# Picking the rows of the ten small expert blocks on the chip instead of loading them

## What is computed

```python
def moe(h, w_router, b_router, w_gate, w_up, w_down):
    t = h.reshape(b * l, d)                       # 384 x 1024
    scores = jax.nn.sigmoid(t @ w_router)         # 16 experts
    ...                                           # best of 4 groups, top 2 in it -> gates
    hidden = jax.nn.silu(einsum('nd,edf->nef', t, w_gate)) * einsum('nd,edf->nef', t, w_up)
    out = jnp.einsum('nef,efd->nd', hidden * gates[..., None], w_down)
```

## Time and profile before

| | |
|---|---|
| runs of the kernel before | 1582.39, 1579.22, 1567.40 us, median 1579.22 us |
| span of the profiled execution | 1581.7 us |
| its own time | not given apart; the run nearest above the span is 1582.39 us, 0.7 us more |
| busy PE / DVE / ACT / POOL | 86% / 33% / 21% / 10% of the span |
| mean granted TensorE clock | 0.919 of full speed |
| DMA moved | 354.67 MB, mean 224 GB/s |

### The profile page before, as it was taken

How to read it: one execution, slowest core, us unless ns; L and a number is a source line. 1 busy time by engine, 2 the same in 40 slices (tenths; PEclk the granted TensorE clock), 3 DMA queues, 4 the chain that set the end, 5 groups by cost and what they waited for, 6 DMA issues and landing times.

```text
span 1581.7 us, 38798 instructions
## 1 busy us (share of the span) xinstructions
PE 1352.5 (86%) x16856; PEld 916.1 (58%) x16856; DVE 524.0 (33%) x1147; ACT 334.9 (21%) x665; POOL 164.3 (10%) x237
## 2 busy tenths in 40 slices
PE   4978899989889898899788759988899889987872
PEld 1446764458677755899444424445565579954441
DVE  1232453134344673311001024447455441110113
ACT  2222121032222313100000023423443210000001
POOL 2012220012231300100000012010000010000001
PEclk9997899999788998999989978998879899999996
DMA  9856426321110116589999985115313458999994
GB/s 396 317 175 203 145 84 248 129 107 56 55 56 4 56 54 276 206 326 391 385 396 401 417 318 221 54 69 213 139 75 160 170 185 309 401 385 399 403 416 169
DMA packets 42072, 354.67 MB, mean 224 GB/s; under 512 B 5675, under 2 KB 10619, under 8 KB 23632
## 3 DMA queue, kind: packets, MB, share of 16 engines
q1 hardware_dynamic: 21456, 302.11, 48.5%
q0 software_dynamic: 8672, 28.53, 5.3%
q10 hardware_dynamic: 11808, 22.03, 4.3%
HBM read 321.63 MB, written 31.01 MB: 223 GB/s over the span
## 4 chain that ended last, share of the span: by engine, by line
PE 66%; DMA 15%; DVE 8%; issue 7%; ACT 3%; SPq 1%; POOLq 0%; another core or an unknown queue 0%; DVEq 0%; ACTq 0%; POOL 0%
PE PB L647 60%; DMA arena<-in_w_moe 7%; DMA ring<-in_w_moe 6%; PE PB L650 5%; DVE arena L1948 4%; DMA ring<-in_w_mod 2%; ACT arena L1486 1%; DVE small L1961 1%; DVE x L1948 1%; DVE arena L1955 0%; SPq L413 0%; DMA arena<-expert_out,rows_i 0%; DVE arena L1958 0%; ACT L1486 0%; DVE hT L1951 0%
## 5 line engine op out<-in xcount | busy, mean ns | idle before, releaser
L647 PE MATMUL PB<-arena 64*64 64x64 f32 (+6 forms) x9564 | 506.8, 301 | 77.9 <-DMA arena<-in_w_moe 35.0
L647 PEld LDWEIGHTS PB<-arena 64*64 64x64 f32 (+3 forms) x9564 | 399.3, 135 | 181.4 <-issue 67.9
L647 PE MATMUL PB<-ring,hT 128*128 128x512 f32 (+1 forms) x720 | 314.0, 591 | 7.7 <-DVE hT L1951 3.6
L647 PE MATMUL PB<-ring,arena 128*32 128x256 f32 (+2 forms) x3648 | 221.1, 393 | 38.7 <-DMA ring<-in_w_moe 31.8
L647 PEld LDWEIGHTS PB<-ring,hT 128*128 128x128 f32 x720 | 137.1, 193 | 167.6 <-issue 162.2
L647 PEld LDWEIGHTS PB<-ring,arena 128*32 128x32 f32 x3648 | 157.0, 113 | 94.6 <-DMA ring<-in_w_moe 38.6
L1486 ACT ACTIVATE arena<-PB 128x256 f32<-128x256 f32 (+4 forms) x211 | 103.1, 489 | 411.4 <-PE PB L647 356.2
L650 PE MATMUL PB<-cst,arena 128*128 128x128 f32 (+2 forms) x758 | 114.4, 290 | 41.9 <-ACT arena L1486 18.9
L650 PEld LDWEIGHTS PB<-cst,arena 128*128 128x128 f32 (+2 forms) x758 | 87.2, 152 | 87.5 <-issue 47.8
L2371 DVE TENSOR_TENSOR arena<-arena,PB 128x256 f32<-128x256 f32 (+1 forms) x32 | 15.1, 472 | 354.4 <-ACT arena L1747 354.4
L1747 ACT ACTIVATE arena<-PB 128x256 f32<-128x256 f32 (+1 forms) x32 | 13.6, 425 | 370.2 <-PE PB L647 370.2
(11 more groups left out here) (149 smaller groups left out, 922.0 us busy)
## 6 DMA issues: line engine op xcount, KB each, us to landing
ring<-in_w_moe SPq DMA_DIRECT2D x48, 2048.0 KB, 14.9
arena<-in_w_moe SPq DMA_DIRECT2D x48, 2048.0 KB, 15.8
ring<-in_w_mod SPq DMA_DIRECT2D x24, 2048.0 KB, 8.6
ring<-in_w_mix SPq DMA_DIRECT2D x22, 2048.0 KB, 8.2
dispatched<-gate ACTq DMA_DIRECT2D x1, 8320.0 KB, 41.4
arena<-dispatched POOLq DMA_DIRECT2D x20, 256.0 KB, 9.2
expert_out<-gate ACTq DMA_DIRECT2D x1, 3456.0 KB, 15.6
expert_out<-arena ACTq DMA_DIRECT2D x12, 288.0 KB, 10.0
```

Of the source, the lines that this page charges most:

```text
L647: return nc.tensor.matmul(out, lhsT, rhs, start=start, stop=stop, **k)
```

## The change

The ten small blocks no longer read `Xd`. DVE keeps each token's two row numbers as floats (`rowsf`), and a new function `rows_hot` makes a matrix of ones and zeros for one small block: 128 tokens by 64 slots, for three tiles. It uses the two buffers of `hot` in turn. TensorE takes the block's rows by `rows_small`, 24 products, in place of `rows_T`. POOL's loop of small loads (L602) is gone. The scatter to `Xd` stays, as blocks 2 to 5 and the extra blocks read it. On DVE the loop over small blocks is written out, since `rows_hot` takes the block's number as a constant. The start value of the semaphore for loaded rows changes with the number of loads.

```diff
@@ experts, POOL
-                with pool.Fori(FULL // 2, half) as i:
-                    for b in range(2):
-                        pool.wait_ge(*steps_of(L, "xT_p", i, b - 2))
-                        pool.dma_start(xb[0:SMALL, b, :], Xd[bass.ds(i * 2 * SMALL + b * SMALL + FULL * GRP, SMALL), :])\
-                            .then_inc(x_land[b], 16)
@@ TensorE
+            def rows_small(L, l, i, c, b):
+
+                if i is None:
+                    pe.wait_ge(*small_rows(l, c))
+                else:
+                    pe.wait_ge(sem("small_rows"), i * L["k"] + l * (NE - FULL) + c - FULL + 1)
+                pe.wait_ge(*steps_of(L, "xT_v", i, c - 1))
+                pe.wait_ge(*steps_of(L, "xT_a", i, c - 1))
+                pe.wait_ge(*steps_of(L, "hT_v", i, c - L["k"]))
+                for k in range(KD):
+                    for t in range(TILES):
+                        ins = mm(PB[:, k // 4, CAP * (k % 4):CAP * (k % 4) + SMALL], htok[:, t, 128 * k:128 * k + 128],
+                                 hot[:, b, t, 0:SMALL], t == 0, t == TILES - 1)
+                ins.then_inc(L["S"]["xT_p"], 1)
...
-                        rows_T(L, i, c + 1, (n + 1) % 2)
+                        if caps(n + 1) == SMALL:
+                            rows_small(L, l, i, c + 1, (n + 1) % 2)
+                        else:
+                            rows_T(L, i, c + 1, (n + 1) % 2)
@@ route, DVE
+                    ts(place_of[:, 3 * ch:3 * ch + 3], rec[:, 0:3], float(FULL * GRP - 1), None, ALU.subtract, None)
@@ DVE
+            def rows_hot(L, l, c):
+
+                dve.wait_ge(*steps_of(L, "xT_p", None, c - L["k"]))
+                if c > FULL:
+                    dve.wait_ge(*small_rows(l, c - 1))
+                at = rowsf[:, 6:12]
+                ts(at, rowsf[:, 0:6], float(c * SMALL), None, ALU.subtract, None)
+                for t in range(TILES):
+                    out, slots = hot[:, c % 2, t, 0:SMALL], M("slots")[:, 0:SMALL]
+                    ts(out, slots, at[:, t:t + 1], None, ALU.is_equal, None)
+                    ins = V.scalar_tensor_tensor(out=out, in0=slots, scalar=at[:, 3 + t:4 + t], in1=out, op0=ALU.is_equal, op1=ALU.add)
+                    if t == TILES - 1:
+                        ins.then_inc(sem("small_rows"), 1)
+                    else:
+                        step(ins)
@@ experts, DVE
-                for c in (FULL - 1, FULL):
+                for c in (FULL, FULL + 1):
+                    rows_hot(L, l, c)
+                for c in range(FULL - 1, NE - 2):
                     rows_copy(L, None, c + 1, (c + 1) % 2)
-                    out_copy(L, None, c - 1, (c - 1) % 2, CAP)
+                    out_copy(L, None, c - 1, (c - 1) % 2, CAP if c - 1 < FULL else SMALL)
                     hidden_copy(L, None, c, c % 2, CAP if c < FULL else SMALL)
                     hidden(L, None, c + 1, (c + 1) % 2, SMALL)
-                with dve.Fori(FULL // 2, half - 1) as i:
...
+                    if c + 2 > FULL + 1 and c + 2 < NE:
+                        rows_hot(L, l, c + 2)
```

More of the change, by code:

```diff
@@ L160, in build @@
         wrout = sb("wrout", KD * NE)
+        rowsf = sb("rowsf", 4 * TILES)
         gatek = sb("gatek", 2 * TILES)
@@ L348, in steps, with small_rows @@
                 "xT_p", "xT_a", "xT_v", "gu", "silu", "hid", "hT_p", "hT_v", "dn", "y_a", "y_v")}
+        def small_rows(l, c):
+            return sem("small_rows"), l * (NE - FULL) + c - FULL + 1
         def loop(S, base, stride, land, land_base, rows, stores):
@@ L382, in build @@
             base_loop.append(loop(blk, l * NE, 2, [w_land, w_land1], [ring_base, [16 * half * l] * 3],
-                                  (x_land, 16 * ((half - 1) * l - 1)), (y_st, 48 * half * l + 48)))
+                                  (x_land, 16 * ((FULL // 2 - 1) * l - 1)), (y_st, 48 * half * l + 48)))
             ext = [sem(f"ext{l}_w_landed{m}") for m in range(3)]
@@ L2269, in route @@
                 rank, f0, f1, gw, row, ge = w(48), w(48), w(48), w(48), w(48), w(48)
-                cum, xbk, off, ov, rec = w(16), w(16), w(16), w(16), w(4)
+                cum, xbk, off, ov, rec, place_of = w(16), w(16), w(16), w(16), w(4), rowsf[:, 0:6]
                 key, rk, base, cap = w(16), w(16), w(16), w(16)
@@ L2395, in experts @@
                         hidden(L, i, n + 1, (n + 1) % 2, CAP)
-                for c in (FULL - 1, FULL):
+                for c in (FULL, FULL + 1):
+                    rows_hot(L, l, c)
+                for c in range(FULL - 1, NE - 2):
                     rows_copy(L, None, c + 1, (c + 1) % 2)
-                    out_copy(L, None, c - 1, (c - 1) % 2, CAP)
+                    out_copy(L, None, c - 1, (c - 1) % 2, CAP if c - 1 < FULL else SMALL)
                     hidden_copy(L, None, c, c % 2, CAP if c < FULL else SMALL)
                     hidden(L, None, c + 1, (c + 1) % 2, SMALL)
-                with dve.Fori(FULL // 2, half - 1) as i:
[L2402 to L2406, removed]
+                    if c + 2 > FULL + 1 and c + 2 < NE:
+                        rows_hot(L, l, c + 2)
+                rows_copy(L, None, NE - 1, 1)
+                out_copy(L, None, NE - 3, 1, SMALL)
+                hidden_copy(L, None, NE - 2, 0, SMALL)
+                hidden(L, None, NE - 1, 1, SMALL)
                 out_copy(L, None, NE - 2, 0, SMALL)
```

## The result

| | before | after |
|---|---|---|
| runs | 1582.39, 1579.22, 1567.40, 1587.12 us | 1726.70, 1734.94, 1735.48, 1728.56 us |
| median | 1580.81 us | 1731.75 us |
| span of the profiled execution | 1581.7 us | 1724.9 us |
| mean granted clock | 0.919 | 0.883 |

The ratio is 1.096, 95% interval 1.090 to 1.103: slower by 151 us. I had said +23, at most +43. The direction was right, the size was not.

The account below looks back on a forecast made before the run. Small blocks were taken as DMA-bound, the bound turning to TensorE with a DVE step in its chain. +2.2 us at full clock plus 21.0 us of clock falls, 23.2 in all, on 1579.2 gave 1602 us, range 1578 to 1622.

Parts of the forecast that it names:

- Supply: DMA in small blocks: without the row loads 16.6 us instead of 17.3, worth 0.67 us a block if DMA stays the bound.
- The products: TensorE in each small block: 24 row products cost 2.75 us, 1.94 more than the transposes they replace.
- The wait: TensorE's row step waits for DVE's matrix behind the gate and up product: 2.88 us idle a block.
- The sum at full clock: Small-block stretches of both layers, TensorE now the bound: +0.4 and +1.8, together +2.2 us.
- The clock: TensorE's clock falls behind 11 in 16 of 18 new gaps: 12.4 falls of 1.69 us, 21.0 us.
- rival B: Clock falls at all 18 small-block gaps, as thin products follow them: +33 us, 1612 us; chance 0.20.
- What costs nothing: POOL's dropped launches, DVE's written-out passes, later modulation loads: 0; two added `route` instructions hidden, bare 0.8 us in all.
- A: Rival: TensorE's clock stays up behind the small-block gaps, making the change a wash: +2.2, 1581 us; chance 0.22.
- C: Rival: `rows_hot` done before TensorE asks, DMA stays the small blocks' bound, full 13.3 us gained: 1566 us; chance 0.05.

Follow-up runs that it names:

- e6: e1 with the ten small-block row loads of the kernel before also issued and awaited, but unused; 1608.52 us, ratio 1.015 to the kernel before.
- e7: Changed kernel with down(c-1) moved ahead of the row products and the matrix wait put before it, so full products follow the gap; 1666.65 us, ratio 1.052.
- e12: Changed kernel with both the short gap of e9 and the order of e7, so full products follow the gap; 1643.62 us, ratio 1.038.
- e9: Changed kernel with the matrix made for one tile in place of three, shortening the gap; all 24 products still run; 1681.09 us, ratio 1.061.
- e8: e1 with every small block's row products run twice, with no gap ahead of them; 1701.59 us, ratio 1.070 to the kernel before.
- e1: Changed kernel with DVE making block c+2's matrix ahead of the hidden copy, blocks 6's and 7's before the loop; 1583.36 us, ratio 1.002.

## Why the prediction was wrong

The mechanism was right as far as it went: the bound turned from DMA to TensorE, with a wait for DVE in its chain. Two terms of the sum were mis-sized: the products, by 55 us, and the falls of the clock, by 77. They are the whole difference between the +23.2 of the prediction and the +155.1 of the stretches. Step by step:

- **Supply** was right: 0.67 us a block from the bytes, 0.6 by the stretches of e6.
- **The products: this step failed.** "48 with 96 columns took 5.49 us, 0.114 each ... so 24 cost 2.75 us" divided a row of one pick (24 products, 48 issues) by two. The pitch per issue was right and does not depend on the columns; a pick costs 5.5 us. For 20 picks that is 55 us that the sum lacked. The code would have shown it: `rows_pick` has 24 products for a block, and the 5.49 us row is that of one block. The Trainium skill, "TensorE: Matmul & The Clock Gate", section "LDWEIGHTS (loading the stationary operand)", gives a load's time as its columns over 1.2, in ns: 107 for 128 columns, so 48 loads would be an estimated 5.1 us. The trace agrees within a tenth (5.5), but the page could not have caught the mistake: 24 loads by it are an estimated 2.6 us, near my 2.75. What was missed is that a pick shows 48 of them.
- **The wait** was right: predicted 2.88 us in 9 blocks of a layer, behind the product of gate and up; measured 54.4 us over 18. `rows_hot` took 1.99 us (779.89 to 781.88) against 1.79.
- **The sum at full clock**: +2.2 with picks of 2.75 us; with 5.5 it is +57.2.
- **The clock: this step failed too, and it is the larger part.** I took 12.4 falls of 1.69 us, 21 us. The rest of the +155.1 us is 98 us, 18 falls of 5.4. Number and price were both too low, because I had read them from gaps ahead of full products. The new gaps are followed by products "with little to stream", which I had written down under rival B and not priced. e7 and e12 put full products back behind the gap, and there a fall costs 1.3 to 2.7 us again. The kernel before does have a stretch of thin products at the low clock, which I did not use, in the router: the same 16 issues without and with a gap ahead of them (the clock had fallen at the gap before that one, of 2.73 us).

```profile
610.99 1.85 PE L647 MATMUL PB<-wrout,hT 128*128 128x16 f32 x16
...
619.60 3.57 PE L647 MATMUL PB<-wrout,hT 128*128 128x16 f32 x16 [2.17 <-ACT hT L1486]
```

  That is 1.72 us more for 16 issues, so an estimated 5.2 for the 48 of a pick, close to the 5.4 measured. The Trainium skill, "TensorE: Matmul & The Clock Gate", section "Why this matters for your kernels", asks that idle gaps be kept below a length that the gaps of e9 do not reach. The trace disagrees: gaps of at most 1.93 us made 12 falls there. Thin products alone do not do it either, as 96 thin issues in a row made none (e8). Falls of this number and price take both.
- **What costs nothing**: the written-out passes of DVE and the later loads of the next layer cost nothing that can be seen; e1 has them and stands at 1.002.
- **The rivals**: B had the right number of falls, but at 1.69 us each; A and C did not occur. C's condition, `rows_hot` done before TensorE asks, is e1. It gave no gain, since C too rested on 2.75 us: with 5.5 a pass is 16.5 us, against 16.6 of supply.

Together: 2.2 + 55 (products) + 98 (falls) = 155 us.

## What to carry to other kernels

Before a row's time is divided by its count, find the code that issued it and check how many instructions make one count. A wait that a change puts on a TensorE that is the bound cost little more than its own length where full products stood behind it (65 us for 56.1, 43 for 34.1); ahead of thin ones it cost 2.8 times that (152 for 54.4 us, 91 for 32.3), so move the producer earlier, or put full work between wait and thin products. And a transfer removed is worth little where the engine that replaces it was itself near its limit: pick where that engine had slack, and leave the rest.

## What was not expected of the hardware

- Gaps of 1.65 to 1.93 us lowered the granted clock in 12 of 18 cases with 48 thin issues behind them; the same with full products behind gave 3.
- After a fall the clock stayed at 0.50 for all the thin issues that were left and returned only within the full products behind them: 48 issues took 8.9 to 10.1 us in place of 5.5. Without a gap 96 thin issues ran at 1.00.
- The fall can come after the work has begun again: at 806.53 us the pick started at 1.00, and 1.1 us later the clock was at 0.50.
- In these traces an f32 product with 128x128 stationary counts as two issues and takes 0.23 to 0.24 us, with 16, 64 or 96 columns moving.
